# A transformer forward pass in one launch: stage boundaries handled per half of the tokens

## The chip, the cores and the metric

The kernel runs on one core of a Trainium2 chip. The metric is the device time of one launch in microseconds (us). Median of three runs of the kernel before: 1211.17 us (1210.68 to 1213.23). The engines are named as the profile names them: PE (TensorE, the matmuls), PEld (its weight loads, which run beside them), DVE (VectorE), ACT (ScalarE), POOL (GpSimd), SP (the queue that issues the transfers). TensorE's clock has two levels, 1.2 and 2.4 GHz; a granted clock of 1.00 is the upper one, 0.50 the lower.

## What is computed

256 tokens (T) of 1024 channels (D), float32, go through two blocks. The first has two layers, with the second layer reading K and V that were made behind the first:

```python
h = rms_norm(x, mix_pre_g[0]);  m = pool_mixer(h)              # causal averages over 2, 4, 8, 16 tokens
x = x + rms_norm(m, mix_post_g[0])
x = x + rms_norm(sq_relu_mlp(rms_norm(x, mlp_pre_g[0])), mlp_post_g[0])      # 1024 -> 4096 -> 1024
k, v = split(rms_norm(x, kv_norm_g) @ w_kv)
q = rms_norm(x, mix_pre_g[1]) @ w_q
x = x + rms_norm(stick_breaking_attention(q, k, v) @ w_o, mix_post_g[1])     # 16 heads of 64
x = x + rms_norm(sq_relu_mlp(rms_norm(x, mlp_pre_g[1])), mlp_post_g[1])
```

The second block: a projection `w_in` to 3072 columns behind a norm, a short gated convolution beside a differential attention with 4 heads, `w_out`, then a router and 32 experts (two of them per token, hidden width 512). `rms_norm(x, g)` is `x * rsqrt(mean(x*x) + 1e-6) * g`; `sq_relu_mlp` squares the ReLU between its two matrices.

## The kernel before

**Staging.** There is no loop over tokens: all 256 stand in SBUF as two halves of 128 (`x[:, s, :]`, s = 0, 1). The weights come as chunks of 2 MB, numbered in the order of use (`N_MLP`, `N_KV`, `N_WO`, `N_IN`, ...), into a ring of four slots (`load`, L474). The load of chunk n waits until chunk n - 4 is split. The second block's 96 expert chunks go into a ring of eight slots; they are loaded ahead as far as slots come free and are then consumed at the rate of the transfers.

**Split matmuls.** A chunk is used in four quarters. Each is taken apart into a rounded part `w_hi` (ACT, L1050) and the rest `w_lo` (DVE, L1338), both f32r. There are four buffers of quarters; a quarter is split two quarters ahead of its use (`AHEAD = 2`, `ahead_of`), and the split of a quarter waits until the buffer's former one has been used (`quarters_used`). `mm3` (L590) makes each product from three matmuls (L593, L594, L595): hi x hi, hi x lo, lo x hi.

**Two forms of product.** `channel_major` (L616) takes 128 output channels of a quarter as the stationary operand and moves 256 tokens: 8 x 3 matmuls of 128 x 128 weights with 256 columns. The token-major forms (down passes, V, WO, WOUT) have a half of the tokens stationary and move 512 channels.

**An MLP** (`mlp`, L660, L1088, L1379) has eight pairs of chunks, two per turn of its loop. An up chunk makes 512 hidden channels in four quarters; ACT takes the ReLU (L1101), ACT and DVE square it and split the square (L1103, L1392, L1395). A down chunk adds 4 quarters x 2 halves x 2 x 3 matmuls of 512 columns onto `acc`, four PSUM banks which were zeroed ahead of the loop (L663 to L666), with the quarter as the outer loop: quarter f is needed 12 matmuls behind quarter f - 1.

**A boundary** is what lies between the last matmul of one stage and the first of the next. Around it every engine has its order written out by hand:

- `post_norm` (ACT L1022, DVE L1306): both halves' squares and sums are taken out of `acc` (ACT), `mg = acc * row` (DVE; times the square of the norm's scale `rstd2` behind an MLP), then `rsqrt` for both halves (mean on DVE, Ln and Exp on ACT, three Newton steps on DVE), and `add_to_x` (L1297) for both.
- behind MLP 0 and MLP 1 the sum of squares of x and a second `rsqrt` follow, and `h = x * rstd` (`normalise`, L1292). Into an MLP x itself is turned, without its scale: the ReLU's square lets it be applied at the end, through `rstd2`.
- `transposes` (L605): 16 PE transposes of 128 x 128 turn x or h into four PSUM banks; a bank holds two channel blocks for all tokens.
- `take_hT` (ACT L1033, DVE L1327): `hT_hi` and `hT_lo` from each bank, times the norm's gain; for K/V/Q a second set, `mixT_hi` and `mixT_lo`, with the other norm's gain.
- the first `channel_major` waits for the first bank (L636); in an MLP all four are awaited (L668).

The projections behind MLP 0 (L694 to L712) run K's eight quarters, Q's eight, V's eight; ACT copies K and Q out of PSUM (L1118, L1120). `project` (L762) is WO and WOUT. The first 4 of the 32 steps from L855 are w_in's first chunk.

## Time and profile before

| | |
|---|---|
| median of three runs | 1211.17 us |
| the profiled execution, span | 1211.6 us |
| PE busy | 1003.6 us (83%) in 5977 matmul instructions |
| PEld busy | 721.4 us (60%) |
| DVE busy | 490.4 us (40%) |
| ACT busy | 378.7 us (31%) |
| mean granted clock | 0.913 |
| transfers | 310.29 MB, mean 256 GB/s |

The stages, by the timeline: front (pooling, its projection) until 41 us, MLP 0 until 222, boundary and K/Q/V until 305, attention until 368, WO until 390.5, MLP 1 from 402.4 to 583.7, w_in to w_out from 597.7 to 728, router until 750, experts until 1205, output. All engines' rows share one clock of microseconds from the span's start. A timeline row "x8" merges eight equal instructions; its duration is that of all of them. Matmuls overlap, so the time of one in a series is read from start to start, not from its own duration. "[3.25 <-DVE hT_lo L1325]" is 3.25 us in which the engine stood idle ahead of the row, ended by DVE's write of hT_lo at line 1325.

### The profile page before, as it was taken

How to read it: one execution, taken by the hardware profiler on the slowest of the kernel's cores; microseconds unless marked ns; L12 is line 12 of the kernel's file. 1: busy time of each engine (PE TensorE's matmuls, PEld its weight loads, DVE VectorE, ACT ScalarE, POOL GpSimd, SP SyncE). 2: the span in 40 equal slices, each digit the busy share in tenths (PEclk: the TensorE clock that was granted, in tenths of full speed). 3: DMA queues.
4: the chain of work that ended last, by engine and by line, in shares of the span. 5: the costliest groups of instructions: out<-in, count | busy, mean ns of one | idle time of the engine just before them, and what ended most of it. 6: DMA issues, size and time to landing. Idle time of an engine off the chain costs nothing.

```text
span 1211.6 us, 15034 instructions
## 1 busy us (share of the span) xinstructions
PE 1003.6 (83%) x5977; PEld 721.4 (60%) x5977; DVE 490.4 (40%) x769; ACT 378.7 (31%) x656; POOL 1.9 (0%) x7
## 2 busy tenths in 40 slices
PE   5799999699999899999698886877666777677773
PEld 4799899598667799899588764333131313131311
DVE  3656656645354656556657764220202010101010
ACT  3545545544244545545454532000000000000000
POOL 0000000000000000000000000000000000000000
PEclk9899999899699899999899998998788878787877
DMA  9555555365003345545150585899999999999994
GB/s 360 179 203 183 181 191 182 112 204 206 8 1 138 115 181 206 183 164 208 70 203 7 209 320 236 346 420 421 422 421 421 421 422 421 422 422 422 422 421 173
DMA packets 93159, 310.29 MB, mean 256 GB/s; under 512 B 2496, under 2 KB 3520, under 8 KB 92992
## 3 DMA queue, kind: packets, MB, share of 16 engines
q1 hardware_dynamic: 92688, 308.17, 65.4%
q0 software_dynamic: 432, 1.57, 0.4%
q8 instruction: 28, 0.46, 0.1%
q14 instruction: 11, 0.09, 0.0%
HBM read 308.68 MB, written 1.05 MB: 256 GB/s over the span
## 4 chain that ended last, share of the span: by engine, by line
PE 57%; DMA 16%; SPq 11%; DVE 10%; ACT 4%; issue 2%; DVEq 0%
PE ps L593 13%; PE ps L594 13%; PE ps L595 13%; SPq L554 11%; DMA ring<-in_w_exp_up 8%; DMA ring<-in_w_exp_down 7%; PE ps L957 4%; PE ps L940 3%; PE ps L969 2%; DVE w_lo L1352 1%; PE ps L977 1%; DVE hT_lo L1325 1%; PE ps L721 1%; PE ps L742 1%; ACT h L1007 1%
## 5 line engine op out<-in xcount | busy, mean ns | idle before, releaser
L1338 DVE TENSOR_TENSOR w_lo<-ring,w_hi 128x1024 fp32r<-128x1024 f32 x162 | 195.3, 1224 | 114.0 <-ACT w_hi L1050 114.0
L593 PE MATMUL ps<-hT_hi,w_hi 128*128 128x256 f32 x736 | 212.5, 289 | 10.0 <-DVE hT_lo L1325 7.7
L594 PE MATMUL ps<-hT_lo,w_hi 128*128 128x256 f32 x736 | 210.3, 286 | 0.0
L595 PE MATMUL ps<-hT_hi,w_lo 128*128 128x256 f32 x736 | 210.2, 286 | 0.0
L1050 ACT ACTIVATE w_hi<-ring 128x1024 fp32r<-128x1024 f32 x162 | 168.9, 1053 | 73.5 <-PE ps L595 67.5
L957 PE MATMUL ps<-ring,x 128*32 128x512 f32 x992 | 143.1, 726 | 52.0 <-DMA ring<-in_w_exp_up 43.1
L593 PEld LDWEIGHTS ps<-hT_hi,w_hi 128*128 128x128 f32 x736 | 143.3, 195 | 13.5 <-issue 11.0
L594 PEld LDWEIGHTS ps<-hT_lo,w_hi 128*128 128x128 f32 x736 | 143.3, 195 | 0.8 <-issue 0.2
L595 PEld LDWEIGHTS ps<-hT_hi,w_lo 128*128 128x128 f32 x736 | 143.3, 195 | 0.0
L969 PE MATMUL ps<-ring,moe 128*32 128x512 f32 x512 | 82.7, 783 | 57.7 <-DMA ring<-in_w_exp_down 56.3
L957 PEld LDWEIGHTS ps<-ring,x 128*32 128x32 f32 x992 | 33.9, 126 | 155.2 <-issue 80.6
L593 PE MATMUL ps<-w_hi,aT_hi 128*128 128x512 f32 x256 | 99.8, 390 | 0.0
L594 PE MATMUL ps<-w_lo,aT_hi 128*128 128x512 f32 x256 | 99.8, 390 | 0.0
L595 PE MATMUL ps<-w_hi,aT_lo 128*128 128x512 f32 x256 | 99.6, 389 | 0.0
L969 PEld LDWEIGHTS ps<-ring,moe 128*32 128x32 f32 x512 | 16.4, 130 | 116.2 <-DMA ring<-in_w_exp_down 78.0
L940 PEld LDWEIGHTS ps<-moe,h 128*128 128x128 f32 x256 | 62.2, 334 | 5.8 <-DVE moe L1653 3.4
L1667 DVE COPY x<-ps 128x512 f32<-128x512 f32 x8 | 5.5, 692 | 146.6 <-PE ps L969 146.6
L940 PE MATMUL ps<-moe,h 128*128 128x128 f32 x256 | 61.5, 401 | 3.3 <-DVE moe L1653 3.3
L1101 ACT ACTIVATE rT<-ps 128x256 f32<-128x256 f32 x64 | 24.6, 384 | 120.6 <-PE ps L595 120.6
L1392 DVE TENSOR_TENSOR aT<-rT 128x256 f32<-128x256 f32 x64 | 27.2, 426 | 66.8 <-ACT rT L1101 66.8
L595 PEld LDWEIGHTS ps<-w_hi,aT_lo 128*128 128x128 f32 x256 | 48.1, 188 | 10.1
L593 PEld LDWEIGHTS ps<-w_hi,aT_hi 128*128 128x128 f32 x256 | 48.1, 188 | 9.6
(245 smaller groups left out, 1121.1 us busy)
## 6 DMA issues: line engine op xcount, KB each, us to landing
ring<-in_w_exp_down SPq DMA_DIRECT2D x32, 2048.0 KB, 22.9
ring<-in_w_exp_gate SPq DMA_DIRECT2D x31, 2048.0 KB, 22.8
ring<-in_w_exp_up SPq DMA_DIRECT2D x31, 2048.0 KB, 23.0
ring<-in_w_up SPq DMA_DIRECT2D x16, 2048.0 KB, 7.9
ring<-in_w_down SPq DMA_DIRECT2D x16, 2048.0 KB, 7.8
ring<-in_w_in SPq DMA_DIRECT2D x6, 2048.0 KB, 8.6
ring<-in_w_kv SPq DMA_DIRECT2D x4, 2048.0 KB, 9.2
ring<-in_w_q SPq DMA_DIRECT2D x2, 2048.0 KB, 9.7
```

Of the source, the lines that this page charges most:

```text
L554: sp.dma_start(dst, src).then_inc(loaded, 16)
L593: mm(out, a_hi, b_hi, start=start, stop=False, skip_group_check=True)
L594: mm(out, a_hi, b_lo, start=False, stop=False, skip_group_check=True)
L595: return mm(out, a_lo, b_hi, start=False, stop=stop, skip_group_check=True)
L721: mm(z[:, 0:T], kT[r:r + 64, m, 0:P], qT[r:r + 64, m, :], start=True, stop=False, skip_group_check=True)
L940: last = mm(wk(2 + k // 4)[:, (k % 4) * P:(k % 4 + 1) * P], h[:, s, k:D:KD], G[:, s, :], start=(s == 0), stop=(s == TT - 1))
L957: last = mm(wk(c // 4)[q, :], xgT[:, k, q], w[:, j, kk, :], start=(k == 0), stop=(k == KD - 1))
L969: last = mm(wk(2 + half)[q, :], actT[:, f, q], w[:, j, half * COLS:(half + 1) * COLS], start=(f == 0), stop=(f == 3))
L1050: fn(w_hi[:, f, :].rearrange("p (k w) -> p k w", k=KD), src, ACT.Copy).then_inc(hi_ready, 1)
L1101: fn(rT[:, f, :], wk(f)[:, 0:T], ACT.Relu).then_inc(relu_ready, 1)
L1338: ve.tensor_tensor(w_lo[:, f, :].rearrange("p (k w) -> p k w", k=KD), src, w_hi[:, f, :].rearrange("p (k w) -> p k w", k=KD).bitcast(F32), ...
L1392: ve.tensor_tensor(aT[:, f, :], rT[:, f, :], rT[:, f, :], ALU.mult).then_inc(sq_full, 1)
```

## The change

Four boundaries (front to MLP 0, MLP 0 to K/V/Q, WO to MLP 1, MLP 1 to w_in) run per half of the tokens:

- **Ahead of the boundary.** Every down pass, in all turns of the loop, and WO's second chunk have the half as the outer loop and the quarter as the inner one. Half 0 of `acc` is done (`half_done`) while PE works on half 1. A quarter's buffer comes free in the pass of half 1.
- **The norm.** `post_half`, `post_mean`, `post_rsqrt`, `post_add` do for one half, in pieces of 512 columns, what `post_norm` did for both.
- **The turn.** `turn_half` turns one half into two PSUM banks with eight transposes; `take_half` takes each half's 8 blocks of 128 x 128 (they were 8 of 128 x 256).
- **Behind the boundary.** `channel_half` does the four quarters of the first chunk first for half 0, then for half 1: 8 x 24 matmuls with 128 moving columns, in place of 4 x 24 with 256. The second half is turned behind three of half 0's quarters; at the front ahead of them; at w_in behind all four.
- **K/V/Q.** x is turned instead of h. The scale is applied on leaving PSUM: for K and Q by a row `rows` that holds rstd of each token in every partition (two f32 matmuls of `ones` and a diagonal, then ACT's copy), on DVE; for V by DVE's scale per partition. ACT no longer copies K and Q.
- **The accumulator's zeroing** moves from ahead of the transposes to behind the first up pass. The MLP loop is turned: the first up pass stands ahead of it, the last down, up, down behind it.
- **Order on ACT and DVE.** At each boundary the next chunk's four splits, which were ahead by two, stand between the pieces of the norm.

The core of the diff:

```diff
+HALVES = (8, 9, 17)
@@ PE
+            def turn_half(src, s, ready, count, bank):
+                pe.wait_ge(ready, count)
+                for k in range(KD):
+                    last = nc.tensor.transpose(ps[:, bank + k // 4, (k % 4) * P:(k % 4 + 1) * P], src[:, s, k:D:KD], ident)
+                    if k % 4 == 3:
+                        last.then_inc(hT_banks, 1)
+            def channel_half(out, b, s, turn, fresh=True):
+                w = [q[:, b, :].rearrange("p (k w) -> p k w", k=KD) for q in (w_hi, w_lo)]
+                t = slice(s * P, (s + 1) * P)
+                for k in range(KD):
+                    if k % 4 == 0:
+                        pe.wait_ge(hT_lo_ready, 4 * turn + 2 * s + k // 4 + 1)
+                    last = mm3(out[:, t], [q[:, k, :] for q in w], [q[:, k, t] for q in (hT_hi, hT_lo)],
+                               s == 0 and k == 0 and fresh, s == 1 and k == KD - 1)
+                if s == 1:
+                    last.then_inc(quarters_used, 1)
@@ PE, mlp
+                def down(j, i):
+                    for s in range(TT):
+                        for f in range(4):
+                            if s == 0:
+                                split(n0 + 2 * j + 1, f, i)
+                                pe.wait_ge(sq_ready, i * (4 * PAIRS) + (32 * layer + 4 * j + f + 1))
+                            for half in range(2):
+                                last = mm3(acc[:, s, half * COLS:(half + 1) * COLS],
+                                           [q[:, f, s * P:(s + 1) * P] for q in (aT_hi, aT_lo)],
+                                           [q[:, f, half * COLS:(half + 1) * COLS] for q in (w_hi, w_lo)], False, False)
+                            if s == 1:
+                                last.then_inc(quarters_used, 1)
+                            elif f == 3:
+                                last.then_inc(half_done, 1)
+                turn_half(x, 0, x_ready, x_count - 1, 0)
+                if layer == 0:
+                    turn_half(x, 1, x_ready, x_count, 2)
+                for s in range(TT):
+                    for f in range(4):
+                        if s == 0:
+                            split(n0, f)
+                        channel_half(wk(f), f, s, turn)
+                        if s == 0 and f == 2 and layer:
+                            turn_half(x, 1, x_ready, x_count, 2)
                 for s in range(TT):
                     for half in range(2):
                         mm(acc[:, s, half * COLS:(half + 1) * COLS], zero_t[:, 0:P], zero_t[:, 0:COLS],
                            start=True, stop=True)
+                with pe.Fori(0, PAIR_ITERS - 1) as i:
+                    down(0, i)
+                    up(1, i)
+                    down(1, i)
+                    up(0, i + 1)
+                down(0, PAIR_ITERS - 1)
+                up(1, PAIR_ITERS - 1)
+                down(1, PAIR_ITERS - 1)
@@ PE, K/V/Q
+                    if s == 1 and f == 2:
+                        pe.wait_ge(diag_ready, 2)
+                        for c in range(TT):
+                            last = mm(wk(2)[:, T + c * P:T + (c + 1) * P], ones, diag[:, c, :], start=False, stop=True,
+                                      skip_group_check=True)
+                        last.then_inc(rows_done, 1)
@@ PE, w_in
+            turn_half(h, 0, h_ready, 3, 4)
+            for s in range(TT):
+                for f in range(4):
+                    if s == 0:
+                        pe.wait_ge(lo_ready, 4 * (N_IN - 1) + f + 1)
+                    channel_half(ps[:, f // 2, f % 2 * T:f % 2 * T + T], f, s, 3, f % 2 == 0)
+                if s == 0:
+                    turn_half(h, 1, h_ready, 4, 6)
@@ ACT
+            def edge_to_mlp(edge, chunks, n, turn, gain, scale):
+                post_half(edge, chunks, 0, scale)
+                post_rsqrt(edge, 0)
+                for f in range(3):
+                    split(n, f, quarter(n, f))
+                take_half(turn, 0, 0, gain)
+                post_half(edge, chunks, 1, scale)
+                split(n, 3, quarter(n, 3))
+                post_rsqrt(edge, 1)
+                pre_half(edge, 0)
+                take_half(turn, 1, 2, gain)
+                pre_half(edge, 1)
+                pre_rsqrt(edge, 0)
+                pre_rsqrt(edge, 1)
@@ ACT, w_in
+            post_half(2, N_IN, 0, rstd2s)
+            post_rsqrt(2, 0)
+            split(N_IN, 0, quarter(N_IN, 0))
+            pre_half(2, 0)
+            pre_rsqrt(2, 0)
+            split(N_IN, 1, quarter(N_IN, 1))
+            post_half(2, N_IN, 1, rstd2s)
+            take_half(3, 0, 4, 4)
@@ DVE
+            def edge_to_mlp(edge, chunks, n, turn, gain, scaled2):
+                post_half(edge, chunks, 0, scaled2)
+                post_mean(edge, 0)
+                post_add(edge, 0)
+                split(n, 0, quarter(n, 0))
+                post_half(edge, chunks, 1, scaled2)
+                take_half(turn, 0, 0, gain)
+                for f in (1, 2):
+                    split(n, f, quarter(n, f))
+                post_mean(edge, 1)
+                post_add(edge, 1)
+                split(n, 3, quarter(n, 3))
+                take_half(turn, 1, 2, gain)
+                pre_half(edge, 0)
+                pre_half(edge, 1)
@@ DVE, K/V/Q
+                if t >= 2:
+                    ahead(n, f)
+                if t == 0:
+                    dve.wait_ge(rows_ready, 1)
+                dve.wait_ge(quarters_used, 4 * n + f + 1)
+                if t < 8:
+                    ve.tensor_tensor(kT[:, t, :], wk(f)[:, 0:T], rows[:, :], ALU.mult).then_inc(proj_taken, 1)
```

## Rows read from the trace of the kernel before

**Rows 1.** Windows: stretch; us; PE, PEld, DVE, ACT, POOL busy; clock; DMA; GB/s
```profile
41.00:222.00 181.00, 180.91 (x1152) 165.42 (x1152) 105.05 (x133) 89.98 (x132) 0.00 (x0) 0.99 0.52 182
...
222.00:241.50 19.50, 9.04 (x60) 8.66 (x61) 14.08 (x31) 12.79 (x31) 0.53 (x1) 0.74 0.18 64
...
750.00:1205.00 455.00, 325.71 (x1904) 129.83 (x1904) 62.73 (x100) 26.57 (x64) 0.00 (x0) 0.85 0.97 397
```

**Rows 2.** Timeline behind MLP 0: start, us, engine, line, operation, [idle before]
```profile
221.53 0.39 PE L595 MATMUL ps<-w_hi,aT_lo 128*128 128x512 f32 x1
...
222.06 2.48 DVE L1318 SCALAR_TENSOR_TENSOR mg<-ps,rstd,row 128x1024 f32<-128x1024 f32 x2 [3.23 <-PE ps L595]
...
225.96 2.48 DVE L1301 SCALAR_TENSOR_TENSOR x<-mg,rstd,x 128x1024 f32<-128x1024 f32 x2
...
234.24 3.03 ACT L1041 ACTIVATE hT_hi<-ps,packed 128x256 fp32r<-128x256 f32 x8 [3.87 <-PE ps L612]
...
235.11 3.23 DVE L1325 SCALAR_TENSOR_TENSOR hT_lo<-ps,packed,hT_hi 128x256 fp32r<-128x256 f32 x8 [2.70 <-ACT hT_hi L1041]
...
236.13 0.36 PE L593 MATMUL ps<-hT_hi,w_hi 128*128 128x256 f32 x1 [0.66 <-DVE hT_lo L1325]
```

**Rows 3.** Timeline, the three other boundaries (front, WO, MLP 1)
```profile
33.93 3.62 PE L612 MATMUL ps<-consts,x 128*128 128x128 f32 x16 [3.90 <-DVE x L1301]
...
40.81 0.57 PE L593 MATMUL ps<-hT_hi,w_hi 128*128 128x256 f32 x1 [3.25 <-DVE hT_lo L1325]
...
390.52 2.36 DVE L1316 TENSOR_TENSOR mg<-ps,row 128x1024 f32<-128x1024 f32 x2 [3.19 <-PE ps L595]
...
402.42 0.44 PE L593 MATMUL ps<-hT_hi,w_hi 128*128 128x256 f32 x1 [3.16 <-DVE hT_lo L1325]
...
405.86 0.35 PE L594 MATMUL ps<-hT_lo,w_hi 128*128 128x256 f32 x1
...
583.68 2.48 DVE L1318 SCALAR_TENSOR_TENSOR mg<-ps,rstd,row 128x1024 f32<-128x1024 f32 x2 [3.23 <-PE ps L595]
...
597.73 0.36 PE L593 MATMUL ps<-hT_hi,w_hi 128*128 128x256 f32 x1 [0.65 <-DVE hT_lo L1325]
```

**Rows 4.** Timeline of PE, first two matmuls of a down pass in MLP 0
```profile
98.75 0.40 PE L593 MATMUL ps<-w_hi,aT_hi 128*128 128x512 f32 x1
98.98 0.40 PE L594 MATMUL ps<-w_lo,aT_hi 128*128 128x512 f32 x1
```

**Rows 5.** Timeline of ACT and DVE, splits at the start of that down pass
```profile
99.69 3.07 ACT L1050 ACTIVATE w_hi<-ring 128x1024 fp32r<-128x1024 f32 x3
...
100.76 3.50 DVE L1338 TENSOR_TENSOR w_lo<-ring,w_hi 128x1024 fp32r<-128x1024 f32 x3 [0.45 <-ACT w_hi L1050]
```

**Rows 6.** Timeline of PE, a restart behind a late split, K projection
```profile
242.65 0.39 PE L593 MATMUL ps<-hT_hi,w_hi 128*128 128x256 f32 x1 [0.41 <-DVE w_lo L1338]
242.88 0.28 PE L594 MATMUL ps<-hT_lo,w_hi 128*128 128x256 f32 x1
243.00 0.28 PE L595 MATMUL ps<-hT_hi,w_lo 128*128 128x256 f32 x1
```

**Rows 7.** Weight loads of two lines: ns min/median/max, first and last start
```profile
L957 PEld LDWEIGHTS ps<-ring,x x992: 106/110/178, 759.0 to 1173.7; 128*32 128x32 f32 x199
...
L722 PEld LDWEIGHTS ps<-strictr,identr x16: 186/186/287, 307.1 to 361.2; 128*128 128x128 f32 x16
```

**Rows 8.** Timeline of PE: attention's f32r matmul, its follower; the router's transposes
```profile
308.64 0.33 PE L722 MATMUL ps<-strictr,identr 128*128 128x128 f32 x1
308.89 0.48 PE L723 MATMUL ps<-qbuf,kbuf 64*128 64x128 f32 x2
...
729.24 2.29 PE L612 MATMUL ps<-consts,x 128*128 128x128 f32 x16 [1.31 <-DVE x L1556]
```

**Rows 9.** Windows of PE: stretch, us, busy, clock, DMA share, GB/s
```profile
315.00:320.00 5.00, 5.00 (x16) 0.50 0.00 0
...
234.00:236.00 2.00, 1.47 (x7) 0.66 0.00 0
```

More of the change, by code:

```diff
@@ L760, in _, with project @@
                     weighted(i - 3)
-            def project(m):
-                for s in range(TT):
+            def project(m, tokens=range(TT)):
+                for s in tokens:
                     for half in range(2):
@@ L769, in project @@
                                    m == 0, m == KD - 1)
-                last.then_inc(quarters_used, 1)
+                if 1 in tokens:
+                    last.then_inc(quarters_used, 1)
+                elif m == KD - 1:
+                    last.then_inc(half_done, 1)
             pe.wait_ge(prob_ready, HEADS)
-            for m in range(KD):
-                split(N_WO + m // 4, m % 4)
+            for m in range(4):
+                split(N_WO, m)
                 if m % 2 == 0:
@@ L779, in _ @@
                 project(m)
-            pe.wait_ge(mg_ready, 4)
-            pe.wait_ge(ss_ready, 12)
+            pe.wait_ge(oT_ready, KD)
+            for s in range(TT):
+                for m in range(4, KD):
+                    if s == 0:
+                        split(N_WO + 1, m % 4)
+                    project(m, [s])
             mlp(1, 2, 6)
-            transposes(h, h_ready, 6)
             def mean_squares(i):
@@ L1044, in split, with take_half @@
+            def take_half(turn, s, bank, gain):
+                for b in range(2):
+                    act.wait_ge(hT_banks, 4 * turn + 2 * s + b + 1)
+                    for k in range(4 * b, 4 * b + 4):
+                        last = fn(hT_hi[:, k, s * P:(s + 1) * P], ps[:, bank + b, (k % 4) * P:(k % 4 + 1) * P], ACT.Copy,
+                                  scale=gains[:, gain, k:k + 1])
+                    last.then_inc(hT_hi_ready, 1)
             def split(n, f, src, i=0):
@@ new lines, in _ @@
+            take_half(0, 0, 0, 0)
+            for f in (2, 3):
+                split(1, f, quarter(1, f))
+            take_half(0, 1, 2, 0)
+            pre_norm(2)
+            mlp(0)
+            act.wait_ge(r2_ready, 1)
+            edge_to_mlp(0, N_MLP[0] + 16, N_KV, 1, 1, rstd2s)
+            for k in range(KD):
+                last = fn(mixT_hi[:, k, :].rearrange("p (s t) -> p s t", s=TT),
+                          ps[:, k // 4:4:2, (k % 4) * P:(k % 4 + 1) * P], ACT.Copy, scale=gains[:, 2, k:k + 1])
@@ L1114, in _ @@
+            last.then_inc(q_hi, 1)
+            for t in range(2, 16):
                 n, f = N_KV + t // 4, t % 4
                 ahead(n, f)
-                act.wait_ge(quarters_used, 4 * n + f + 1)
-                if t < 8:
-                    fn(kT[:, t, :], ps[:, f, 0:T], ACT.Copy).then_inc(proj_taken, 1)
-                else:
-                    fn(qT[:, t - 8, :], wk(f)[:, 0:T], ACT.Copy, scale=DH ** -0.5).then_inc(proj_taken, 1)
+                if t == 3:
+                    act.wait_ge(rows_done, 1)
+                    fn(rows[:, :], wk(2)[:, T:2 * T], ACT.Copy).then_inc(rows_ready, 1)
@@ new lines, in pre_mean, with pre_half, take_half @@
+            def pre_mean(edge, s):
+                dve.wait_ge(pre_squares, 2 * edge + s + 1)
+                ve.tensor_scalar(ms[:, s:s + 1], ss[:, s:s + 1], EPS, None, ALU.add).then_inc(pre_ms, 1)
+            def pre_half(edge, s):
+                pre_mean(edge, s)
+                dve.wait_ge(pre_r0, 2 * edge + s + 1)
+                newton(s)
+            def take_half(turn, s, bank, gain):
+                for b in range(2):
+                    dve.wait_ge(hT_hi_ready, 4 * turn + 2 * s + b + 1)
+                    for k in range(4 * b, 4 * b + 4):
+                        t = slice(s * P, (s + 1) * P)
+                        last = lower(hT_lo[:, k, t], ps[:, bank + b, (k % 4) * P:(k % 4 + 1) * P], gains[:, gain, k:k + 1],
+                                     hT_hi[:, k, t])
+                    last.then_inc(hT_lo_ready, 1)
@@ L1406, in _ @@
+            for n in (N_KV + 4, N_KV + 5):
                 for f in range(4):
```

329 lines of the change are left out of this document (209 added, 120 removed).

## The prediction

> **What bounds the kernel now.** I read the busy time by stage first, then the timeline of each boundary, then one steady pair of MLP chunks, then weight loads by size. Two things bound the time. In both MLPs the matmul engine (PE) is busy 180.9 of 181 us, at full clock; in the expert stage the transfers are (DMA share 0.97) [rows 1]. The expert stage starts when everything ahead of it is done, and all its early loads are released by points of the stages ahead, so a microsecond won or lost ahead of it is won or lost in the total. Between the stages PE starves: of the 19.5 us from 222 to 241.5 it works 9.0 [rows 1], because the norm goes through ACT and DVE over both token halves before it can turn the next operand [rows 2].
>
> The gaps, from the end of PE's issue (0.30 us before DVE takes the result, by 221.53 + 0.23 and 222.06 in [rows 2]) to the first matmul of the next stage: 221.76 to 236.13 = 14.4; 390.22 to 402.42 = 12.2; 583.38 to 597.73 = 14.35; and 3.25 us of idleness ahead of 40.81 [rows 2, 3]. That is all the change can win: 44 us, 3.7% of the span.
>
> **Prices.** Matmuls follow each other every 0.119 us with 256 columns moving and every 0.227 with 512 [rows 4, 6]; an up pass has 96 of the first kind, 11.4 us, a down pass 48 of the second, 10.9. DVE needs 0.40 us for 256 columns (3.23/8) and 1.24 for 1024 (2.48/2) [rows 2]; a line through both gives 0.26 for 128 and 0.68 for 512. ACT needs 0.38 for 256 (3.03/8) [rows 2]; with 1.02 for 1024 (a third of 3.07) [rows 5] 0.27 for 128 and 0.6 for 512; for a sum I add 0.15.
>
> **The narrow matmuls decide.** The change splits the first four quarters behind each boundary into halves: 8 x 24 = 192 matmuls with 128 moving columns in place of 96 with 256. Every one still loads 128 x 128 weights. What does such a one cost? The trace has none in a row. Its moving part alone would be 0.119 - (0.227 - 0.119)/2 = 0.065. But the weight load takes 110 ns for 32 columns and 186 for 128 [rows 7]: 0.8 ns per column, so 0.10 us for 128 beside a fixed latency. At 256 columns the 0.107 of moving hides it; at 128 it can't. Transposes, which move 128 columns against 128 x 128 weights, took 2.29 us for 16 at full clock [rows 8]; less the last one's 0.27 and some 0.2 us for the second half of x that is 0.115 each. The f32r matmul with 128 columns whose load can't run ahead (the one before uses half the rows) is followed after 308.89 - 308.64 = 0.25 [rows 8]; that is load plus moving plus a drain, and the upper bound. The bounds are 0.065 and 0.25 (which would add 100 us to the forecast); I take 0.119, since the load's 0.10 to 0.11 is as long as what paces the wide ones. So each boundary's 192 cost 22.9 us where 96 cost 11.4: **+11.4 us of PE at each of four boundaries**, 46 in all, against 44 of gaps.
>
> The Trainium skill speaks to this. Its page "TensorE: Matmul & The Clock Gate", section "Back-to-back issue gap", gives about 81 ns per matmul at 128 columns for a sustained stream with loads. An estimate with that figure: 15.6 us a boundary and a total near the time before (rival B). The same page's LDWEIGHTS section has the load scale with the number of columns, and the trace agrees [rows 7].
>
> **One boundary in the new order (MLP 0 to K/V/Q).** Let 0 be the end of the last chunk's first half; PE works on the second until 24 x 0.227 = 5.45. Squares and product of half 0 in 512-column pieces: 0.25 to 1.85; mean, Ln, Exp, Newton 1.3 (as before); x half 0 at 4.4. DVE splits quarter 0 until 5.65 and takes half 1's product until 7.0. PE turns half 0 at 5.45 to 6.4; ACT takes it 6.1 to 8.3 (8 x 0.27), DVE half a bank later: **first matmul 8.35**, not 14.4 + 5.45 = 19.8. Three quarters of half 0 (72 x 0.119) end at 16.9. Meanwhile ACT squares half 1 (to 9.9), DVE splits quarters 1 and 2 (to 11.9), then mean, rsqrt and add: x half 1 at 14.5. Not late, so PE turns it 16.9 to 17.9, does quarter 3 until 20.8 (hT of half 1 is there), and half 1 until 32.2, with 0.45 for the two f32 products of ones and diag. DVE's first K product waits for that row (ACT's copy at 30.5), with the splits of the next chunk queued behind it; the first lands at 32.6, the next at 35.0: about 0.3 of wait. Then 12 quarters of 2.86 and V's 96 x 0.227 as before. End 89.1; before it was 19.8 + 16 x 2.86 + 21.8 and 1.2 of late splits (the largest in [rows 6]) = 88.5: **+0.7**, rounded up. The K copies move from ACT to DVE (1.7 us a quarter with the split, under 2.86): nothing. If that cover were gone it would be 0.4 each.
>
> **WO to MLP 1.** Same chain; first up pass done at 32.2, then the four zeroing matmuls, formerly in the gap, on the path: +0.9, so 33.15. Before: 5.45 + 12.2 + 11.4 + 1.6 for 17 matmuls at 1.2 GHz, 0.21 instead of 0.12 [rows 3] = 30.65. **+2.5.**
>
> **MLP 1 to w_in.** Here h must be normalised ahead of the turn. h half 0 at 7.35; ACT then has half 1's squares ahead of the take (until 10.2), so DVE has the first bank lowered at 12.4. All of half 0 runs until 23.9; only then PE turns half 1 (to 24.85), and waits for ACT and DVE until 26.75. End 38.2; before 5.45 + 14.35 + 11.4 + 0.5 = 31.7. **+6.5**, and 1 more for the clock, which the hole of 4 us can bring to 1.2 GHz, as the longer gaps did [rows 3]; ends 0 and 3: **+7.5**.
>
> **Front to MLP 0.** Before: first matmul 40.81, 15 of them at 1.2 GHz (+1.4 by the same price), up pass done at 53.6. Both turns are done at 37.6 as before [rows 3]; half 0 starts then rather than at 40.81, and half 1 (ready at 43) follows: 37.6 + 22.9 + 0.9 of zeroing = 61.4. **+7.8.**
>
> **Every down pass.** Each is now halves outside, quarters inside, so PE needs the down chunk's third quarter after 12 matmuls (2.72 us), not 24. Around D = 98.75: ACT finishes the last relu and square, then splits quarter 2 (from 99.69), and DVE's part of it runs 100.76 to 101.99 [rows 5], at D + 3.24. PE stands 0.56 us, and by the restart behind such a stand (0.23 to the next in place of 0.12) 0.11 more [rows 6]. Quarter 3 lands at D + 4.4, needed at 4.75; the next chunk's quarter 0 becomes free 4.1 us before the pass ends and needs 2.5. So 0.67 for each of 14 passes (in the first of each MLP zeroing covers it): **+9.4**. Bounds 0 and 16 x 0.9 = 14.
>
> Sum: 7.8 + 0.7 + 2.5 + 7.5 + 9.4 = 27.9. The profiled execution spans 1211.6 us, the median is 1211.2, so the same is added to it: **1239 us**. Rows, DMAs from POOL (released once x half 1 is there) and SP are not late: a chunk is 8 us in transfer and 22 of PE.
>
> **Rivals.**
> B, the narrow ones cost their moving part (0.065): the other side. For: nothing in the trace forbids loads faster than their latency suggests. Against: the load's slope and the transposes [rows 7, 8]. Half 0's quarters then wait for DVE's splits (11.9, 15.7), so the boundaries give front -2.4, K/V/Q -5.3, MLP 1 -6.0, w_in -0.4 and passes +9.4: **-4.7, 1207**. It is won from a price below about 0.075; at 0.081 it gives +2, 1213. Chance 0.19, of which 0.13 is faster by over 0.2% (about what a measurement here can tell from none) and 0.06 within it.
> C, narrow matmuls let the clock fall. Attention ran at 1.2 GHz for some 20 us, of which one window stands here, with PE busy throughout [rows 9]. Each boundary that falls costs 192 x 0.095 = 18 more: 1257 with one, 1312 with all. Against: the clock rose in a boundary while PE did nothing but transposes, which are as narrow (mean 0.66 there, full behind) [rows 9]. Chance 0.11.
> D, the down passes don't wait (ACT and DVE a little sooner): **1230**. Chance 0.12.
> The forecast A, 1229 to 1250 with the bounds of the hole and the waits: 0.58. The range reaches from B's 1207 to 1262, which leaves out most of C. Faster 0.13, same 0.06, slower 0.81.
>
> **What the profile after would show.** 388 or so more PE instructions; the 128-column group of the three matmul lines at an interval near 0.12 (its start to start), not 0.065; busy share of PE up while the time is longer; idle time of PE ahead of the down group of about 0.45 x 14, released by DVE's w_lo; gaps at the boundaries of 2 us, but of 2 and 4 at w_in. I am wrong if narrow ones come every 0.08 or less, or if the clock there is 1.2 GHz.

## The result, and the profile after

The changed kernel takes 1305.2 us (1293.5 to 1317.2, four runs), the kernel before 1210.9 beside it: a ratio of 1.0743, 95% interval 1.0708 to 1.0777. Ratios here leave out runs in a slow state of the clock (of these four the one at 1317.2 us), while the medians have every run, so that the two don't divide exactly. It is slower, as forecast, but by 94 us (90 by the ratio) and not by 28, and outside the range. The profiled execution spans 1299.1 us, 87.5 more than the one of before.

The page first: engines, the span in 40 slices, and two of the transfers.

```profile
PE 1089.7 (84%) x6365; PEld 802.8 (62%) x6365; DVE 505.1 (39%) x849; ACT 383.2 (29%) x697; POOL 1.9 (0%) x7
...
PEclk9999999669789799999759998898888888888887
...
GB/s 357 144 192 187 190 145 191 145 51 208 65 1 130 82 157 167 194 194 168 137 20 130 1 292 332 190 409 409 409 409 409 409 410 410 410 410 410 410 409 167
...
ring<-in_w_exp_down SPq DMA_DIRECT2D x32, 2048.0 KB, 23.8
```

PE has 388 instructions and 86 us more of busy time, and its clock row holds dips that don't end with the gaps (slices 8 and 9, 20 and 21). The second thing is at the other end: the expert stage streams at 409 to 410 GB/s. In the kernel before the same slices stood at 420 to 422, with 22.9 us to the landing of such a chunk:

```profile
GB/s 360 179 203 183 181 191 182 112 204 206 8 1 138 115 181 206 183 164 208 70 203 7 209 320 236 346 420 421 422 421 421 421 422 421 422 422 422 422 421 173
...
ring<-in_w_exp_down SPq DMA_DIRECT2D x32, 2048.0 KB, 22.9
```

The timeline of PE in the kernel after, at the points that close each stage (columns as in [rows 2]):

```profile
37.12 0.30 PE L611 MATMUL ps<-hT_hi,w_hi 128*128 128x128 f32 x1 [0.42 <-DVE hT_lo L1513]
37.26 0.28 PE L612 MATMUL ps<-hT_lo,w_hi 128*128 128x128 f32 x1
37.37 0.28 PE L613 MATMUL ps<-hT_hi,w_lo 128*128 128x128 f32 x1
...
59.57 0.39 PE L611 MATMUL ps<-w_hi,aT_hi 128*128 128x512 f32 x1
...
232.77 1.04 PE L638 MATMUL ps<-consts,x 128*128 128x128 f32 x8
235.85 0.30 PE L611 MATMUL ps<-hT_hi,w_hi 128*128 128x128 f32 x1 [2.04 <-DVE hT_lo L1513]
...
237.54 0.41 PE L611 MATMUL ps<-hT_hi,w_hi 128*128 128x128 f32 x1
237.75 0.42 PE L612 MATMUL ps<-hT_lo,w_hi 128*128 128x128 f32 x1
...
249.70 1.93 PE L638 MATMUL ps<-consts,x 128*128 128x128 f32 x8
...
337.75 0.45 PE L788 MATMUL ps<-qbuf,kbuf 64*128 64x256 f32 x1 [1.59 <-DVE vbuf L1656]
...
422.93 1.04 PE L638 MATMUL ps<-consts,x 128*128 128x128 f32 x8
426.01 0.30 PE L611 MATMUL ps<-hT_hi,w_hi 128*128 128x128 f32 x1 [2.04 <-DVE hT_lo L1513]
...
438.96 1.93 PE L638 MATMUL ps<-consts,x 128*128 128x128 f32 x8
...
455.80 0.39 PE L611 MATMUL ps<-w_hi,aT_hi 128*128 128x512 f32 x1
...
631.09 1.16 PE L638 MATMUL ps<-consts,h 128*128 128x128 f32 x8 [2.10 <-DVE h L1688]
636.17 0.45 PE L611 MATMUL ps<-hT_hi,w_hi 128*128 128x128 f32 x1 [3.92 <-DVE hT_lo L1513]
...
660.15 0.48 PE L611 MATMUL ps<-hT_hi,w_hi 128*128 128x128 f32 x1 [1.54 <-DVE hT_lo L1513]
```

The gaps are what the chain of the forecast gave: the first matmul comes 3.08 us after the end of MLP 0 and after the end of WO, 2.04 of them idle, where it came after 14.4 and 12.2 [rows 2, 3]. The 128-column matmuls follow each other every 0.11 us (37.26, 37.37) while the clock is full. But at 237.54 the interval becomes 0.21, and it stays there. Windows of the kernel after, with the columns of [rows 1]: stretch; us; PE, PEld, DVE, ACT and POOL busy; granted clock; DMA share; GB/s.

```profile
235.85:277.70 41.85, 41.85 (x204) 41.85 (x205) 14.08 (x37) 13.84 (x35) 0.53 (x1) 0.52 0.21 64
426.00:440.50 14.50, 14.49 (x80) 14.50 (x81) 6.13 (x12) 3.70 (x11) 0.53 (x1) 0.59 0.46 148
440.50:455.00 14.50, 14.50 (x123) 14.50 (x122) 8.28 (x26) 7.90 (x21) 0.00 (x0) 0.94 0.09 35
636.10:656.60 20.50, 20.43 (x96) 20.46 (x96) 6.44 (x16) 3.86 (x8) 0.00 (x0) 0.50 0.30 103
660.10:680.80 20.70, 20.64 (x97) 20.65 (x97) 5.05 (x16) 2.32 (x3) 0.00 (x0) 0.50 0.00 1
```

Ahead of K/V/Q the narrow matmuls run at 0.52 for 41.85 us, ahead of w_in at 0.50 for both halves; behind WO the first half runs at 0.59 and the second at 0.94; at the front all 192 ran at the full clock (37.12 to 58.59, 0.112 each). PE is busy throughout: the stretches are slow, not idle.

Stage by stage, from the end of PE's issue in one stage to that in the next, profiled executions, us:

| stage | before | after | difference | of it low clock | rest | forecast |
|---|---|---|---|---|---|---|
| front and MLP 0 | 221.8 | 232.8 | +11.0 | 0 | +11.0 | 7.8 + 4.7 |
| K/V/Q, to attention's first matmul | 84.7 | 105.0 | +20.3 | 20.9 | -0.6 | 0.7 |
| attention and WO | 83.7 | 85.2 | +1.4 | 1.4 | 0 | 0 |
| MLP 1 | 193.1 | 205.9 | +12.8 | 6.4 | +6.4 | 2.5 + 4.7 |
| w_in to w_out | 144.4 | 172.7 | +28.3 | 22.3 | +6.0 | 6.5, clock 1 |
| router | 22.1 | 22.2 | +0.1 | 0 | +0.1 | 0 |
| experts and output | 461.7 | 475.4 | +13.7 | 0 | +13.7 | 0 |

The clock's part is worked out from starts of matmuls. In K/V/Q the stretch from the first narrow matmul to the last took 41.9 us (235.85 to 277.78), and 22.9 in e3, the run below in which it kept the full clock; the 96 wide ones behind it took 13.4 and 11.6: 20.9 together. Behind WO the first 72 took 12.95 instead of 8.1, eight transposes and eight more matmuls 1.5 more: 6.4. At w_in 192 took 41.0 instead of 21.5, the next 48 7.6 instead of 5.8, the transposes between 0.9 more: 22.3. So of 87.5 us about 51 are the clock, 14 the experts, and 23 what the forecast had counted (27.9, of which 1 was for the clock).

### The profile page after: what moved, and what is told of

Its sections match the earlier page's. It is cut to its first block, busy times and chain, and to the rows that moved or that the text cites. A ratio compares the mean times of both kernels' runs of the same rounds, so it can differ in the third digit from the quotient of the medians.

```text
span 1299.1 us, 15827 instructions
## 1 busy us (share of the span) xinstructions
PE 1089.7 (84%) x6365; PEld 802.8 (62%) x6365; DVE 505.1 (39%) x849; ACT 383.2 (29%) x697; POOL 1.9 (0%) x7
## 4 chain that ended last, share of the span: by engine, by line
PE 59%; DMA 21%; DVE 9%; ACT 5%; SPq 5%; issue 2%; ACTq 0%; DVEq 0%
PE ps L611 14%; PE ps L613 14%; PE ps L612 14%; DMA ring<-in_w_exp_down 13%; DMA ring<-in_w_exp_up 8%; SPq L572 5%; PE ps L1039 4%; PE ps L1051 2%; PE ps L1022 2%; DVE w_lo L1518 1%; DVE w_lo L1532 1%; ACT w_hi L1148 1%; PE ps L1059 1%; PE ps L788 1%; PE ps L809 1%
## 5 line engine op out<-in xcount | busy, mean ns | idle before, releaser
L611 PE MATMUL ps<-hT_hi,w_hi 128*128 128x256 f32 (+1 forms) x864 | 266.7, 309 | 11.7 <-DVE hT_lo L1513 10.0
L612 PE MATMUL ps<-hT_lo,w_hi 128*128 128x256 f32 (+1 forms) x864 | 264.7, 306 | 0.0
L613 PE MATMUL ps<-hT_hi,w_lo 128*128 128x256 f32 (+1 forms) x864 | 264.6, 306 | 0.0
L1518 DVE TENSOR_TENSOR w_lo<-ring,w_hi 128x1024 fp32r<-128x1024 f32 x164 | 198.9, 1223 | 113.2 <-ACT w_hi L1148 109.5
L611 PEld LDWEIGHTS ps<-hT_hi,w_hi 128*128 128x128 f32 x864 | 188.4, 218 | 14.3 <-issue 10.9
L612 PEld LDWEIGHTS ps<-hT_lo,w_hi 128*128 128x128 f32 x864 | 188.5, 218 | 0.8 <-issue 0.2
L613 PEld LDWEIGHTS ps<-hT_hi,w_lo 128*128 128x128 f32 x864 | 188.2, 218 | 0.0
L611 PEld LDWEIGHTS ps<-w_hi,aT_hi 128*128 128x128 f32 x256 | 48.1, 188 | 21.5 <-issue 9.1
L612 PEld LDWEIGHTS ps<-w_lo,aT_hi 128*128 128x128 f32 x256 | 48.1, 188 | 9.1
## 6 DMA issues: line engine op xcount, KB each, us to landing
ring<-in_w_exp_down SPq DMA_DIRECT2D x32, 2048.0 KB, 23.8
ring<-in_w_exp_up SPq DMA_DIRECT2D x31, 2048.0 KB, 23.8
```

The source lines that it names most:

```text
L611: mm(out, a_hi, b_hi, start=start, stop=False, skip_group_check=True)
L612: mm(out, a_hi, b_lo, start=False, stop=False, skip_group_check=True)
L613: return mm(out, a_lo, b_hi, start=False, stop=stop, skip_group_check=True)
L1518: ve.tensor_tensor(w_lo[:, f, :].rearrange("p (k w) -> p k w", k=KD), src, w_hi[:, f, :].rearrange("p (k w) -> p k w", k=KD).bitcast(F32), ...
```

## The experiments

Theory at the start: an idle hole, however short, lets the clock fall behind it, and narrow matmuls don't raise it again; rival: narrow matmuls let it fall by themselves. And for the experts: the new tensors move the buffers that the chunks land in. The first three runs take away the holes, the narrow matmuls and the waits of the down passes, one at a time.

**e1: the holes filled.** Products of zeros go where PE would wait; they compute nothing that is used.

```diff
+            def fill(n):
+                for _ in range(n):
+                    mm(wk(3), zero_t[:, 0:P], zero_t[:, 0:COLS], start=True, stop=True)
...
             turn_half(x, 0, x_ready, 3, 0)
+            fill(9)
             for s in range(TT):
...
+            fill(9)
             turn_half(h, 0, h_ready, 3, 4)
+            fill(17)
```

> The changed kernel, with dummy products of zeros (f32r, 128 x 512, into an unused PSUM bank) where PE stands idle at three boundaries: 9 behind the first turn of K/V/Q and of MLP 1, 9 ahead of and 17 behind the first turn of w_in. No wait is changed. Theory A (the idle hole lets the clock fall to 1.2 GHz, and the narrow matmuls behind it do not raise it again, but would not have let it fall by themselves): the granted clock stays near 1.00 in all three narrow stretches, as it did at the front where PE came straight from its transposes; about 19 us less behind MLP 0, 7 behind WO and 25 behind MLP 1, so 1301 falls to about 1250. Theory B (128-column matmuls themselves let the clock fall): the clock falls some microseconds into each stretch all the same, and the time stays within 10 us of 1301.

Measured: 1279.0 us (1253.0 to 1282.7), where 1250 was expected. The windows of PE in e1 (columns here and in the next ones as in [rows 9]: stretch, us, busy, clock, DMA share, GB/s):

```profile
31.20:82.40 51.20, 49.71 (x220) 0.50 0.26 97
244.00:290.00 46.00, 45.61 (x348) 1.00 0.36 120
642.10:666.00 23.90, 23.63 (x110) 0.50 0.06 24
```

With the hole filled, K/V/Q's narrow stretch keeps the full clock, and WO's did too. At w_in the first half kept it; the clock fell at 642.1, behind the one hole that I had left open (1.94 us ahead of the second half). But the front, which was at full clock in the kernel after, now was low from 31.2 on: the stretch that is low is not the same in each build. Three of the four runs lie at 1279 to 1283 us, at a mean clock of 0.91; the fourth, at 1253.0 and 0.938, is near the expectation, but its profile wasn't taken.

**e2: first products wide again.** Both halves are turned first, then 256 columns; everything else of the change stays.

```diff
-                        channel_half(wk(f), f, s, turn)
...
+                turn_half(x, 1, x_ready, x_count, 2)
+                pe.wait_ge(hT_lo_ready, 4 * turn + 4)
+                up(0, 0)
```

> The changed kernel with the halves kept in the norm, the residual, the turn and the down passes, but the first four quarters behind each boundary multiplied once with 256 columns, after both halves are turned. Theory A: the narrow matmuls are the loss, by their weight loads (10 us at each of four boundaries) and by the clock (51 us in all). Then the first matmul comes at about 17.5 us behind the end of half 0 in place of 19.8 before, the down passes still wait 0.67 us each, and the whole is 1215 to 1230. Rival: something else in the halved boundaries (more and smaller ACT and DVE work, waits behind the splits) costs the time: then it stays above 1270.

Measured: 1247.6 us (1247.3 to 1249.2), ratio to before 1.0296 (1.0279 to 1.0313). It wins back 57.6 us of the 94, more than the 40 of PE work that the narrow halves cost (4 x 10.1, by 192 x 0.112 and 96 x 0.119), though its gaps are about as long as before's (K's first matmul 13.3 us behind the end of MLP 0). Low periods around the gaps are 7 to 17 us long instead of 44 and 51: in e2 the clock was back 4 to 6 us after the first wide matmul. But 1215 to 1230 was expected, and this missed it: the expert stage's 14 us were still in, and the wide matmuls ran some 20 us of their time at the low clock, where before's ran 7.

**e3: down passes by quarters.** The narrow boundaries stay; of the down passes only the last of each MLP goes half by half.

```diff
-HALVES = (8, 9, 17)
+HALVES = (1, 2, 3)
...
-                    down(0, i)
+                    down_q(0, i)
                     up(1, i)
-                    down(1, i)
+                    down_q(1, i)
```

> The changed kernel with the quarter as the outer loop again in every down pass but the last of each MLP. The forecast's step says 0.67 us of waiting for the third quarter's split in each pass: 12 passes less of it, 6 to 9 us less than the changed kernel, and PE's idle time ahead of the down group falls from 6.4 us to about 1. If the waits only hid other lateness, no change.

Measured: 1268.7 us (1266.7 to 1293.1), ratio 1.0466 (1.0444 to 1.0488). The group of the down passes' first matmuls, in the kernel after and in e3:

```profile
L611 PE MATMUL ps<-w_hi,aT_hi 128*128 128x512 f32 x256 | 101.4, 396 | 6.4 <-DVE w_lo L1518 6.4
```

```profile
L611 PE MATMUL ps<-w_hi,aT_hi 128*128 128x512 f32 x256 | 100.0, 391 | 0.8 <-DVE w_lo L1531 0.8
```

The idle time, 6.4 us in 16 passes, goes to 0.8. 6 to 9 us were expected, and that and the restarts are 9; but the profiled execution is 34 us shorter than after's. The other 25 are mostly the clock: in e3 K/V/Q's narrow stretch ran at full speed although the hole of 2.04 us was there (at 231.12 where after has 235.85). So a hole of 2 us doesn't always bring the fall. What differs ahead of it is that all down passes of e3 but the last have no stands of 0.4 us; whether that is the reason isn't shown.

**e4: narrow matmuls in the kernel before.** K's and w_in's first four quarters are multiplied in two halves of 128 columns, at the same place, behind the old gap.

```diff
+                for s in range(TT):
+                    t = slice(s * P, (s + 1) * P)
+                    for k in range(KD):
...
+                        last = mm3(out[:, t], [q[:, k, :] for q in w], [q[:, k, t] for q in (hT_hi, hT_lo)],
...
-                if t < 8:
-                    channel_major(ps[:, f, 0:T], f, (hT_hi, hT_lo), ready=hT_tile(1) if t == 0 else None)
+                if t < 4:
+                    channel_narrow(ps[:, f, 0:T], f, ready=hT_tile(1) if t == 0 else None)
...
```

> The kernel before with one thing of the change: the first four quarters of K and of w_in are multiplied in two halves of 128 columns each, quarter by quarter, after everything is turned as before. Price of the weight loads alone: 96 more matmuls at each of two places, 192 x 0.112 - 96 x 0.119 = 10 us each, 1231 in all, clock at 1.00 there as before (it has risen by the time they start). If 128-column matmuls let the clock fall by themselves: up to 18 us more at each, 1250 to 1267, with windows of 0.50 inside the stretch.

Measured: 1272.0 us (1269.6 to 1282.3), ratio 1.0509 (1.0455 to 1.0564), +61 us for two boundaries. The windows of PE:

```profile
221.70:238.40 16.70, 6.10 (x36) 0.69 0.20 78
238.40:275.20 36.80, 36.80 (x175) 0.50 0.18 58
275.20:288.60 13.40, 13.40 (x98) 0.84 0.32 91
```

192 narrow ones in place of 96 wide are 9.8 us a boundary (21.5 - 11.7), 0.10 us more for each of 175 another 17.8, and the wide tail at 0.84 is 1.7: 29 of the measured 30. The price of the narrow ones and their low clock is here without any other part of the change. The expectation had them at full clock (1231) unless narrow ones let it fall (1250 to 1267); they did fall here, and the time is above both. In the kernel before the wide matmuls start at the same place, behind the same gap of 10 idle us, and stay at full clock. So it isn't the length of the gap that decides, but what follows it.

What raised the clock in the kernel before can be read off its trace. Transposes and windows of PE (as in [rows 9]):

```profile
231.80 3.67 PE L612 MATMUL ps<-consts,h 128*128 128x128 f32 x16 [9.89 <-DVE h L1295]
...
395.60 3.66 PE L612 MATMUL ps<-consts,x 128*128 128x128 f32 x16 [1.39 <-DVE x L1301]
```

```profile
225.10:235.30 10.20, 3.50 (x16) 0.50 0.16 51
235.30:241.50 6.20, 5.54 (x45) 1.00 0.00 0
395.80:399.20 3.40, 3.40 (x16) 0.50 0.25 87
399.20:402.60 3.40, 0.24 (x2) 1.00 0.23 67
402.60:406.00 3.40, 3.40 (x17) 0.50 0.00 0
```

The low period ends where the 16 transposes end, at 235.3 and at 399.2, whether it has lasted 10 us or 3; so it is at the front (37.4) and ahead of w_in (597.2). Transposes have 128 columns too, but of plain f32. They don't always suffice: in e6, e7 and e11 the clock came back only 4 us or so into the wide matmuls of K/V/Q. Nor do they keep it: in e4 it fell again at 238.4, 2.5 us into the narrow ones, and stayed low for them all.

**e7: 400 narrow matmuls in the middle of K/V/Q** of the kernel before, their output unused.

```diff
                         pe.wait_ge(q_lo, 4)
+                        for r in range(400):
+                            mm(wk(3)[:, 0:128], hT_hi[:, r % KD, 0:P], hT_hi[:, (r + 1) % KD, 128:T], start=True, stop=True)
```

> The kernel before with 400 matmuls of 128 x 128 weights and 128 moving columns put between K and Q, on operands that are there, into a bank that is free; results unused. PE has had no idle moment for 40 us there. If narrow matmuls cost 0.112 and keep the clock: +45 us, 1256. If they let the clock fall by themselves (theory A': no hole is needed): the clock falls inside the run and stays low to its end, up to 400 x 0.213 = 85 us, about 1290 with the first microseconds at full clock.

Measured: 1257.5 us (1254.5 to 1259.1), ratio 1.0375 (1.035 to 1.04). The window of PE over the run:

```profile
260.50:305.10 44.60, 44.60 (x403) 1.00 0.05 19
```

44.6 us for the 400 (the window touches three more) is 0.111 each, at the full clock from the first to the last. So narrow ones don't lower it by themselves behind 25 us of steady wide work (24.8 by its trace, not the 40 of the expectation), and the price of one is measured alone. The rival falls in its simple form; what is left is that they may not raise it once it is low.

**e5 and e6: the addresses.** e5 is the changed kernel with ss4, rstd2s and rows (1152 bytes a partition) allocated behind all other tensors, so that the rings lie where they lay before. e6 is the kernel before with 1152 unused bytes ahead of the ring.

```diff
-        ss4 = sb("ss4", [P, 4])
...
-        rstd2s = sb("rstd2s", [P, 2])
-        rows = sb("rows", [P, T])
...
         zero_t = sb("zero_t", [P, COLS], F32R)
+        ss4 = sb("ss4", [P, 4])
+        rstd2s = sb("rstd2s", [P, 2])
+        rows = sb("rows", [P, T])
```

```diff
+        pad = sb("pad", [P, 288])
         ring = sb("ring", [P, RING, CHUNK])
```

> The changed kernel with its three new SBUF tensors (ss4, rstd2s, rows: 1152 bytes a partition) allocated behind everything else, so that the two rings of chunks have the addresses they had before. Not one instruction differs otherwise. In all kernels built on the changed one the expert stage's 2 MB chunks landed in 23.8 us (median) instead of 22.9, and the stage took 14 us more. Theory (the rings' addresses): back to 22.9, 410 to 422 GB/s, 14 us less than the changed kernel in that stage. Rival (the stage's later start, or its own state): 23.8 again.

> The kernel before with an unused SBUF tensor of 1152 bytes a partition allocated ahead of the ring, nothing else. Theory (addresses): expert chunks in 23.8 us and 1211 + 14 = 1225. Rival: no difference, 1211.

Measured: e5 1291.3 us (1281.3 to 1305.9), 13.9 less than after, though the two kernels' runs overlap; e6 1226.1 (1223.2 to 1227.0), ratio 1.0118 (1.0094 to 1.0142), 14 to 15 more than before. In e5 the chunks land in 22.9 us and the stage streams at 421 GB/s, in e6 in 23.8 us at 409. From the router's first transpose to the end it is 482.4 us before, 482.6 in e5 and 482.3 in e12 below, but 496.1 in after and 496.2 in e6, whatever the clock did ahead of it.

**e11 and e12: which bytes.** The kernel before with 128 and with 1024 unused bytes (32 and 256 floats) in the same place.

> The kernel before with one unused tensor of 128 bytes per partition allocated ahead of the expert chunks' ring, nothing else. It tells which part of the 1152 bytes shifts the time of the expert stage. If the small remainder does (the two small tensors' 128 bytes): 1223 to 1227, chunks landing at 23.8 us and 409 GB/s. If the 1024 bytes do: 1211, 22.9 us and 421 GB/s.

> The kernel before with one unused tensor of 1024 bytes per partition ahead of the ring, nothing else. The reverse of the run with 128 bytes: 1211 with chunks at 22.9 us if the alignment left over by 128 bytes is what costs, 1223 to 1227 with chunks at 23.8 us if 1024 bytes do. Both slow: any move of the ring does it, or the address where the ring ends.

Measured: e11 1223.3 us, ratio 1.0104 (1.0086 to 1.0123); e12 1213.2, ratio 1.0016 (0.9998 to 1.0033). The pages' transfers, e11 and then e12:

```profile
GB/s 356 179 202 188 184 179 196 96 207 207 1 1 139 154 168 187 196 191 185 98 145 1 284 332 216 410 409 409 409 409 409 409 410 410 410 410 410 410 409 148
```

```profile
GB/s 360 179 203 182 184 188 182 112 207 202 9 1 138 112 184 205 185 163 208 70 204 6 209 320 236 345 420 421 422 421 421 421 421 422 421 422 422 421 421 174
```

128 bytes cost about what 1152 do, and 1024 cost nothing that stands out. So what counts is not the move but where it leads: a start 1024 bytes on is as good as the old one, and one 128 bytes on from either costs. Whether 256 or 512 bytes would do as well no run tells. The Trainium skill has an account in which it is 256 ("DMA: Bandwidth & Descriptors", section "How a descriptor splits into AXI transactions"): transactions have 256 bytes and start at multiples of 256, so that a descriptor that starts beside such a multiple needs an extra one, with beats of 32 bytes for nothing. An estimate from that page for a 4096-byte packet: 132 beats instead of 128, 3.1%; measured are 421 to 409.5 GB/s, 2.8%.

The trace fits this only in part. In the expert stage (900 to 1150 us) of the kernel before nearly every 4096-byte packet took 159 ns; in after the mean is 164, but 22% still took 159, and 10% took 172. And in MLP 0 (60 to 200 us), where the DMA engines are half idle, 92% of the 4096-byte packets took 159 ns in both kernels, though the ring had moved there too; of the 2048-byte ones 93% took 84 ns before and 79% in after. A fixed price for each packet would show in all of them, and it doesn't. The runs show which shifts cost; the reason stays open, and the page tells of its split for fetched bytes, while here the moved side is the one written.

**e8: wide, by quarters, holes filled, old addresses.** e2's, e3's and e5's edits together, and zero products in the holes of the three boundaries behind MLP 0, WO and MLP 1; the front's stay.

```diff
                 turn_half(x, 0, x_ready, x_count - 1, 0)
...
+                if layer:
+                    fill(33)
+                turn_half(x, 1, x_ready, x_count, 2)
+                if layer:
+                    fill(10)
```

> Everything that the runs point at put right in the changed kernel: 256-column products once both halves are turned (as in e2_wide), quarters outside in all down passes but the last of each MLP (as in e3), the rings at their old addresses, and the idle of PE at the three boundaries filled with products of zeros, so that no real matmul runs at 1.2 GHz. From e2_wide's 1247.6: -14 for the expert chunks, -7 for the down passes, -19 for half of the 44 us at 1.2 GHz that lay under its matmuls: 1207. If the clock theory is wrong it stays near 1226.

Measured: 1216.1 us (1214.1 to 1218.2), ratio 1.0039 (1.0023 to 1.0055); 1207 was expected. Without narrow matmuls, down-pass stands and the shifted ring the change is nearly back at the time before, and no better.

**e9: the whole change, narrow halves and all, with old addresses and every hole filled** (20 zero products at the front, 9 and 9, and 9, 17 and 9 around w_in).

> The whole change with its 128-column products, with the expert chunks' buffers back at the addresses that they had before, and every idle hole of TensorE ahead of a 128-column stretch filled with products of zeros (20 ahead of the front, 9 and 9 behind MLP 0 and WO, 9, 17 and 9 around the w_in boundary); the added products compute nothing that is used. Theory A (the hole drops the clock, the 128-column products only fail to raise it again): the granted clock stays at 1.00 through all four 128-column stretches. Then of after's 87.5 us the clock's part (about 19 at K/V/Q, 7 at WO, 25 at w_in) and the addresses' 14 are gone: 1231 to 1241. Rival B (128-column products lower the clock by themselves within a stage, hole or not): stretches at 0.50 of 40 to 50 us remain, 1265 to 1295.

Measured: 1248.8 us, the four runs 1249.2, 1230.6, 1248.3 and 1249.5, ratio 1.0238 (1.018 to 1.0296). That is between the 1231 to 1241 of the one theory and the 1265 to 1295 of the other; a single run reached the first. The windows of PE over the four narrow stretches of the profiled run, which is the first of these:

```profile
38.20:79.20 41.00, 41.00 (x185) 0.50 0.15 52
254.10:277.00 22.90, 22.90 (x205) 1.00 0.35 117
406.00:439.80 33.80, 33.80 (x256) 1.00 0.39 141
621.10:645.70 24.60, 24.58 (x209) 1.00 0.24 87
```

Three of four stretches hold the full clock from end to end, which none but the front's did in after. The fourth, at the front, fell 2 us after it began and stayed low: 185 x 0.102 = 19 us, just the distance to the run of 1230.6, whose mean clock was 0.932 and not 0.918 (its profile wasn't taken, so that the front held there is inferred). Filling works behind a long busy stretch and isn't certain behind the front, ahead of which PE idles.

**e10: what of the change can pay.** As e8, but the second half's norm goes ahead of the weight splits and of the first half's turn on ACT and DVE, and the turns have PSUM banks of their own:

```diff
                 post_rsqrt(edge, 0)
                 for f in range(3):
                     split(n, f, quarter(n, f))
-                take_half(turn, 0, 0, gain)
                 post_half(edge, chunks, 1, scale)
+                post_rsqrt(edge, 1)
+                take_half(turn, 0, base, gain)
+                take_half(turn, 1, base + 2, gain)
                 split(n, 3, quarter(n, 3))
-                post_rsqrt(edge, 1)
```

> An attempt at a kernel that keeps of the change only what pays: the norms, residuals and turns by token half, but the first products 256 columns wide once both halves are turned; the norm of the second half goes ahead of the splits and of the first half's turn; only the last pass of a down projection and WO go half by half; old addresses; holes filled with products of zeros that compute nothing. Theory: the hole ahead of the first product shrinks from 14.4 us to about 9 behind MLP 0 and WO (-5.5 each), from 14.3 to 12 ahead of w_in (-2), and no low clock follows the holes: 1196 to 1203. Rival: the boundary's chain of ACT and DVE is as long as before and the work that was moved ahead of the splits shows up behind them: 1210 to 1217.

Measured: 1197.8 us (1193.5 to 1203.9), ratio 0.9902 (0.9877 to 0.9928): faster than the kernel before by 12.8 us. The timeline of PE and the row that ends the wait behind MLP 0:

```profile
219.94 1.06 PE L638 MATMUL ps<-consts,x 128*128 128x128 f32 x8
220.75 3.45 PE L644 MATMUL ps<-zero_t 128*128 128x512 f32 x14
...
224.40 1.16 PE L638 MATMUL ps<-consts,x 128*128 128x128 f32 x8 [0.20 <-DVE x L1503]
225.32 2.99 PE L644 MATMUL ps<-zero_t 128*128 128x512 f32 x12
...
228.54 0.39 PE L611 MATMUL ps<-hT_hi,w_hi 128*128 128x256 f32 x1 [0.23 <-DVE hT_lo L1527]
```

The first useful matmul comes 8.6 us behind the end of MLP 0 (14.4 before), 8.4 behind WO (381.13 to 389.57; 12.2 before), 11.9 behind MLP 1 (569.71 to 581.62; 14.35 before). With 2.5 us at the front (the first down pass starts at 51.41, before at 53.91) that is 14.5 of the 14.7 us between the two spans. So the waits are shorter and the matmuls wide, and the sum pays. How much of it is the half-wise norm isn't shown: e10 also fills its holes, and no run fills those of the kernel before. An estimate from its rows: at three boundaries the 16 transposes would take 2.29 us [rows 8] instead of 3.67, and the 32 matmuls at 0.21 would win 3.0, so up to 7 of the 12.8 us might come from filling alone.

## Why the prediction was wrong in size

- **The gaps and the chain in a boundary: right.** First matmul forecast 8.35 us behind the first half's end, 8.5 measured (5.45 + 3.08); waits of 2, and 2, 4 and 1.5 at w_in (forecast 1.9, 4 and 1.9).
- **The price of a narrow matmul: right.** 0.119 taken, 0.112 measured (37.26 on), 0.111 in e7. Rival B with 0.065 is excluded. The Trainium skill's 81 ns for 128 columns ("TensorE: Matmul & The Clock Gate", section "Back-to-back issue gap") isn't reached by these f32r matmuls with a load each; the load's slope of [rows 7] was the better guide. The front came 2.1 us cheaper (59.57 - 53.91 = 5.7, not 7.8), 1.3 of it by this price (192 x 0.007).
- **The down passes: the step held, its two terms were each off a little.** The stand is 0.39 to 0.59, mostly 0.46, and not 0.56 (which by its own rows is 0.52: 101.99 - 98.75 - 2.72); a pass with its restart takes 0.68 to 0.87 more. 14 of them: 10.6, forecast 9.4. Rival D falls.
- **The step that failed: the clock.** The forecast put 1 us of it at w_in and the rest into rival C with a chance of 0.11; the runs show 51 us, and the sign of being wrong that it had named, 1.2 GHz in the narrow stretches. It argued from the one place in [rows 9] where the clock rose while PE did transposes that narrow work raises it, since transposes "are as narrow". The reading of the place was right, and holds at all four boundaries of before; the step from there to these matmuls was not. Of f32r matmuls with 128 columns, PE did 37 us in a row at 1.2 GHz in e4 and 41 in e1 without a rise, while wide ones brought it within 4 to 6 us in e2. The second reading, that a short hole is harmless since a long one was, failed too: behind before's long gaps come 16 transposes and wide matmuls, behind these holes narrow ones. C's price of 18 a boundary was right (20.9 and 22.3 with what stands around the 192).
- **"The expert stage moves rigidly": failed by 13.7 us.** The forecast took the diff's three small tensors for nothing. They move the ring by 1152 bytes, 1024 of which do nothing and 128 cost the whole. There was a row for the rate (397 GB/s in [rows 1]) but none for the address.
- The rests: MLP 1 2.5 forecast, 1.1 measured (6.4 less seven passes, 5.3); w_in 6.5 forecast, 6.0 measured. The sum without clock and addresses was 26.9 against 23 measured, and the narrow price alone takes 5.4 off it (4 x 192 x 0.007). Each of these terms is within 2.1 us of its forecast. e9's best run is 20 over before, with the waits of the down passes still in it; in its profiled run attention's low period was 10 us long and not 20 as before, some 5 us less.
- **Open:** why K/V/Q's and w_in's narrow stretches didn't get the clock back and WO's did. It came back after 13.6 us (428.7 to 442.3 in after, 449.5 to 463.1 in e5, 401.4 to 415.0 in e3), in all three 1 to 1.4 us behind the end of the eight transposes of the second half (438.96 + 1.93 in after); but K/V/Q has the same eight inside its low period (249.70 + 1.93), and stayed low. Also why the front fell in e1, e5 and e9 and not in after, and why e3's hole did no harm. The runs show that 37 and 41 us of narrow f32r work can pass without raising a low clock; they don't give the condition under which it falls or comes back.

## What to carry to other kernels

Ask of every wait of PE what comes behind it. If it is wide matmuls, the low clock is soon over; if it is many small ones, count them at the low clock to their end, whether the wait is short (2 us in after) or long (10 us in e4). Don't take one kind of small matmul for another: transposes and f32r products of the same width did not do the same to the clock. Where a norm is split to shorten the wait, keep the matmuls wide and put the second half's norm ahead of everything that can be late. When an edit adds a buffer, look at where it moves the buffers behind it: here 128 bytes ahead of a large transfer target cost 13 us, and 1024 cost next to nothing.

## What the runs showed of the hardware

- An f32r matmul with 128 moving columns and a 128 x 128 load of its own comes every 0.111 to 0.112 us at 2.4 GHz (e7, the front in after) and every 0.213 at 1.2 (K/V/Q in after); with 256 columns every 0.119. Half the columns save 6% of the time.
- The granted clock stayed at 1.2 GHz through 37 us of narrow f32r matmuls without a break in e4 and 41 in e1's front, and for 44 and 51 us around K/V/Q and w_in in after, where transposes and a hole of 1.5 us lie between; it stayed at 2.4 GHz for 44.6 us of the same matmuls behind wide work (e7).
- In the kernel before the clock rose as the 16 transposes ended at all four boundaries (37.4, 235.3, 399.2, 597.2).
- A ring moved by 128 or 1152 bytes takes 409.5 GB/s where it had 421, with 23.8 us and not 22.9 for 2 MB: 12 to 15 us of this kernel. Moved by 1024 bytes it takes 421.
- The changed kernel's times go with its clock: 1293.5 us at a mean clock of 0.896, 1317.2 at 0.885, a spread of 1.8%; the four runs of the kernel before beside it spread by 0.2%.
